# Splitting the value products of an attention stage over the two partition halves of a PSUM bank

## The chip, the cores and the metric

The kernel runs on one core of a Trainium2 chip. The metric is the device time of one execution in microseconds. The core has TensorE (PE, with weight loads shown apart as PEld), VectorE (DVE), ScalarE (ACT), GpSimd (POOL), and DMA queues that SyncE (SP), ACT and POOL issue to. PE writes only to PSUM (the tile `PS`, 128 partitions by 8 banks of 512 fp32), and DVE and ACT carry results from there to SBUF.

## The reference, cut to what matters

One inference step of a two-layer decoder trunk: a prompt of 1024 tokens with 16 meta tokens ahead of it (1040 rows), and 8 sample sequences of 8 new tokens with 512 cached ones. Layer 0 has a convolution branch and a forgetting attention of 8 heads with 64 channels; layer 1 has a short convolution and causal pooling. Each is followed by a LayerNorm and a SwiGLU feed-forward part. The change touches the prompt's attention alone:

```
s = q @ k.T / 8 + (c_q - c_k)        # c: running sum of the log forget gates
s = where(pos_k <= pos_q, s, -inf)
p = softmax(s)
out = p @ v                          # 64 columns a head
```

## The kernel before, in words

All work is placed by hand: each engine has one list of instructions, and semaphores order the engines among each other. Projections and feed-forward products (lines 688 to 690) are three fp32r matmuls for each product; they take most of the time, before and after the attention stage.

The attention stage is a loop over 80 units, ten for each head, which every engine runs through in its own list. Within a head the order is `ORDER = (0, 1, 2, 3, 4, 5, None, 6, 8, 7)`: a number i is query tile i of the prompt (128 queries, the last of them, i = 8, 16 queries) against key tiles 0 to i; `None` is one sample sequence. Unit u of head h is 10 h + its place, so units 40 to 49 belong to head 4. I write scores(u), peak(u) and so on for unit u's instructions. In step n of the loop the engines do this, in this order:

- PE: scores(n) (lines 847 to 851; for a sample sequence lines 864 to 866); transposes of the probabilities of unit n-2 (line 893); in some steps transposes of cached keys (line 873) and other small products; values(n-3) (line 914, for a sample sequence line 904).
- DVE: the reciprocal of the sum of unit n-1 (line 1686); peak(n), the row maximum (line 1682); a copy of transposed probabilities of unit n-2 to `PT` (line 1695); in some steps a piece of the convolution's norm (line 1751); in the steps 6, 7 and 9 of a head a piece of the next head's queries and keys, `head_low` (lines 1504 and 1711 with 1040 columns, line 1714).
- ACT: exp(n) to `PB` (line 1193); a copy of transposed probabilities (line 1200) or of cached keys to `KTS` (line 1205); in some steps a square for the convolution's norm (line 1267); copy(n-3), the result out of PSUM (line 1222, for a sample sequence line 1220); in the steps 5 to 8 of a head a piece of the next head (line 1239).
- POOL: normalising `PB` of unit n by the reciprocal (line 583).

Transposes and values are fp32. A value product of unit u has the key tile's 128 by 64 values as weights and 128 by m probabilities moving (m is 128, or 16 for i = 8), and adds over the i + 1 key tiles into partitions 0 to 63 of bank 7. One such product stands as two records in the trace. Bank 7 is the only one for values:

```
pe.wait_ge(att_evac, u + 1)     # ahead of values(u): the unit before has left bank 7
dve.wait_ge(exp_done, u + 3)    # ahead of the reciprocal of unit u
gp.wait_ge(rc_ready, u + 1)     # ahead of the normalising of unit u
```

`att_evac` counts the copies of line 1222. After the 80 units DVE takes reciprocals of the convolution's norm (`inverse_conv`, line 1733) and splits the first weights of the output projection into a high and a low part (`split_centred`, line 1515, after ACT's line 1112); then PE begins the output projection.

Of the kernel before, what the change touches and what calls it, by code (L numbers as in the profile page):

```python
# [10 lines left out]
ALU = mybir.AluOpType  # L11
# [3 lines left out]
P = 128  # L15
# [10 lines left out]
NH, HD = 8, 64  # L26
# [46 lines left out]
NU = NH * len(ORDER)  # L73
# [26 lines left out]
def build(nc, t):  # L100

    ctx = ExitStack()
    with ctx:
        def at(name, off, shape, dt=F32):
            n = int(np.prod(shape[1:])) * 4
            assert off % 32 == 0 and off + n <= 229344, (name, off, n)
            return nc.alloc_sbuf_tensor_at(name, shape, dt, offset=off), (off + n + 31) // 32 * 32

        def sem(name):
            return ctx.enter_context(nc.semaphore(name))  # L110

# [12 lines left out]
        AH, o = at("AH", A0, [P, KT, T], F32R)
# [15 lines left out]
        WFH, o = at("WFH", o, [P, KT, NH], F32R)  # L140
        WFL, o = at("WFL", o, [P, KT, NH], F32R)
        LFR, o = at("LFR", o, [P, NPAGE, NS, NH])

        HH, o = at("HH", B0, [P, 2, T], F32R)
        HL, o = at("HL", o, [P, 2, T], F32R)
        Y, o = at("Y", o, [P, KT, T])
        SQ, o = at("SQ", R0, [P, KT, C])
        RSD, o = at("RSD", o, [P, 2, C])
        YSM, _ = at("YSM", R0 + 21984, [P, 2, C])
        YSV, o = at("YSV", o, [P, 2, 2, C])  # L150
        assert o <= R0 + 26400

        SQA, o = at("SQA", B0 + 8 * T * 4, [P, HT, C])
        YSA, o = at("YSA", o, [P, 2, C])
        assert o <= R0

        XIN, o = at("XIN", B0, [P, XB, D])
        XTT, o = at("XTT", o, [P, TB, KT, P])
        PIN, o = at("PIN", o, [R_ALL, HALF])
        SIN, o = at("SIN", o, [P, 2, HALF])  # L160
        assert o <= B0 + 11 * T * 4

        STG, o = at("STG", A0, [P, 4, HALF])
        LFZ, o = at("LFZ", o, [NH, 3, T])
        LFC, o = at("LFC", o, [NH, TP])
        LCH, o = at("LCH", o, [NH, TP], F32R)
        LCL, o = at("LCL", o, [NH, TP], F32R)
# [3 lines left out]
        PB, o = at("PB", A0, [P, 3, TP])  # L171
        RSV, o = at("RSV", o, [P, NC, C])
        assert o <= A0 + 4 * T * 4
        QS1, o = at("QS1", A0 + 4 * T * 4, [P, 2, TP], F32R)
        assert o <= A0 + 6 * T * 4
        QS2, o = at("QS2", A0 + 6 * T * 4, [96, 2, TP], F32R)
        VP, o = at("VP", o, [P, 2, NTT, P])
        PT, o = at("PT", o, [P, 2, 8 * P])
        assert o <= A0 + 12 * T * 4
        RS, o = at("RS", B0 + 10 * T * 4, [64, HALF])  # L180
        KS1, o = at("KS1", A0 + 12 * T * 4, [P, 2, TP], F32R)
        assert o <= A0 + 14 * T * 4
        KS2, o = at("KS2", A0 + 14 * T * 4, [96, 2, TP], F32R)
        assert o <= B0

        KR, o = at("KR", 37504, [P, NPAGE, HALF])
        VR, o = at("VR", o, [P, NPAGE + 1, HALF])
        KTS, o = at("KTS", o, [P, HT, KS])
        QBD, o = at("QBD", o, [P, 328])
        SLS, o = at("SLS", o, [P, 64])  # L190
        QBA, o = at("QBA", o, [32, TP])
        assert o <= A0

        IDR, o = at("IDR", R0 + 24992, [P, P], F32R)
# [10 lines left out]
        MIX, o = at("MIX", B0, [P, HT, ES + T + EP])  # L205
        YEXT, BG, PEXT = MIX[:, :, 0:ES], MIX[:, :, ES:ES + T], MIX[:, :, ES + T:]
        assert (ES + T + EP) * 4 <= 4 * T * 4
        T1, o = at("T1", o, [P, EP + 1])
        T2, o = at("T2", o, [P, EP + 1])
        DH, o = at("DH", o, [P, T], F32R)  # L210
        WMR, _ = at("WMR", o, [P, HT, P])
        DL, o = at("DL", o, [P, T], F32R)
        OSA, o = at("OSA", o, [P, HALF])
        OSB, o = at("OSB", o, [NS * HS, HALF])
        CMP, o = at("CMP", o, [P, NS * HS + NS * NQ])
        assert o <= R0 + 26400
        WMH, o = at("WMH", R0 + 29344, [P, HT, P], F32R)
        WML, o = at("WML", o, [P, HT, P], F32R)
# [3 lines left out]
        PS = ctx.enter_context(nc.psum_tensor("PS", [P, 8, 512], F32))  # L222
# [50 lines left out]
        qk_done, nm_ready, exp_done, rc_ready, pn_ready = (sem("qk_done"), sem("nm_ready"), sem("exp_done"),  # L273
                                                           sem("rc_ready"), sem("pn_ready"))
        ta_done, tb_done, pta_ready, ptb_ready = sem("ta_done"), sem("tb_done"), sem("pta_ready"), sem("ptb_ready")
        pv_done, att_evac, sb_done, sb_evac = sem("pv_done"), sem("att_evac"), sem("sb_done"), sem("sb_evac")
        lfr_in, lfs_in, sel_in, cs_ready, cq_ready, sel_ready = (
            sem("lfr_in"), sem("lfs_in"), sem("sel_in"), sem("cs_ready"), sem("cq_ready"), sem("sel_ready"))
        kr_in, vr_in, kt_new, qbd_zero, qbd_ready, sls_ready = (sem("kr_in"), sem("vr_in"), sem("kt_new"), sem("qbd_zero"),
# [75 lines left out]
        def chunk(c):  # L355
            return slice(c * C, (c + 1) * C)
# [22 lines left out]
        def _(sp):  # L379
# [73 lines left out]
            def residual(k):  # L453

                sp.dma_start(Y[:, k, :], XT[:, k, :]).then_inc(y_in[k], 16)
# [21 lines left out]
            for k in range(KT):  # L477
                if k == 6:
                    sp.wait_ge(sb_evac, NS)
                residual(k)  # L480
            for n in range(4, 8):
                load(2 * ST_OUT0 + n, (2 * ST_OUT0 + n) % 4, out_rows(0, n))
# [199 lines left out]
        def _(pe):  # L682
# [214 lines left out]
            def values(u, h, i, m, n, na, nb):  # L897
                pe.wait_ge(att_evac, u + 1)
                if i is None:
                    pe.wait_ge(pta_ready, na + 2)  # L900
                    pe.wait_ge(vr_in, 80 * (h + 1))
                    for g in range(NPAGE + 1):
                        kw = P if g < NPAGE else NQ
                        mm = pe.matmul(PS[0:64, 7, :], PT[0:kw, u % 2, 64 * g:64 * g + 64], VR[0:kw, g, :], start=(g == 0), stop=(g == NPAGE))  # L904
                    mm.then_inc(pv_done, 1)
                    return
                if u % 20 == 0:
                    pe.wait_ge(vp_ready[h // 2 % 2], 32 * (h // 4 + 1))
                pe.wait_ge(pta_ready, na + (2 if i == 8 else 1) + 1)
                if i > 3:  # L910
                    pe.wait_ge(ptb_ready, nb + 2)
                for jt in range(i + 1):
                    kw = min(P, TP - jt * P)
                    mm = pe.matmul(PS[0:HD, 7, 0:m], VP[0:kw, h // 2 % 2, jt, HD * (h % 2):HD * (h % 2 + 1)], PT[0:kw, u % 2, m * jt:m * jt + m],  # L914
                                   start=(jt == 0), stop=(jt == i))
                mm.then_inc(pv_done, 1)

            def turn_back(s):
# [168 lines left out]
        def _(act):  # L1087
# [129 lines left out]
            def result(u, h, i, m, n, na, nb):  # L1217
                act.wait_ge(pv_done, u + 2)
                if i is None:
                    act.copy(RS[:], PS[0:64, 7, :]).then_inc(att_evac, 1)  # L1220
                else:
                    act.activation(QKV[HD * (h % 2):HD * (h % 2 + 1), h // 2, i * P:i * P + m], PS[0:HD, 7, 0:m], ACT.Copy).then_inc(att_evac, 1)

# [264 lines left out]
        def _(dve):  # L1488
# [9 lines left out]
            def two(ap):  # L1498

                return ap.unsqueeze(1).to_broadcast([P, 2, C])  # L1500
# [187 lines left out]
            def turned(u, h, i, m, n, na, nb):  # L1688
# [8 lines left out]
                if i == 8:  # L1697
                    dve.wait_ge(ta_done, na + 2)
                    dve.tensor_copy(PT[0:META, u % 2, 8 * m:9 * m], PS[0:META, 5, 0:m]).then_inc(pta_ready, 1)

            dve.wait_ge(ab_open, 1)
            def head_low(h, part):

# [31 lines left out]
            for n in range(NU + 3):  # L1735
                if 1 <= n < NU + 1:
                    inverse(*UNITS[n - 1])
                if n < NU:
                    peak(*UNITS[n])
                if 2 <= n < NU + 2:  # L1740
                    turned(*UNITS[n - 2])
                if n == 1:
                    select()
                c = norm_step(n, 13)
                if c is None:
                    c = norm_step(n, 14)
                if c is not None:
                    q = n % 10 - 3
                    qs = slice(2 * q, 2 * q + 2)
                    dve.wait_ge(la_mean, c + 1)  # L1750
                    dve.tensor_tensor(AEXT[:, qs, chunk(c)], AEXT[:, qs, chunk(c)], two(PS[:, 2, 0:C]), ALU.subtract).then_inc(la_cen, 1)
                if n < NU - 10 and n % 10 in (6, 7, 9):
                    head_low(n // 10 + 1, (6, 7, 9).index(n % 10))
                if n > NU:
                    inverse_conv(n - NU - 1)
# [360 lines left out]
```

## Time and profile before

| | us |
|---|---|
| median of 3 runs | 2765.15 (2763.03 to 2765.69) |
| the profiled execution, its own time | 2763.57 |
| its span, first to last instruction | 2761.9 |
| PE busy in the span | 2639.9 (96%) |
| stretch 336 to 633 us, steps 5 to 82 of the attention | 297.00, PE busy 286.99 |
| value products (line 914) in it, PE busy | 88.07 |
| mean granted TensorE clock, span | 0.982 |

A row of the timeline gives the start, the time from there to the end of a run of like instructions, the engine, line and operation, and in brackets the engine's idle time before and what ended it. Ends of matmuls are modelled, so the pace of a run of matmuls is read from its starts.

### The profile page before, as it was taken

How to read it: one execution, taken by the hardware profiler on the slowest of the kernel's cores; microseconds unless marked ns; L12 is line 12 of the kernel's file. 1: busy time of each engine (PE TensorE's matmuls, PEld its weight loads, DVE VectorE, ACT ScalarE, POOL GpSimd, SP SyncE). 2: the span in 40 equal slices, each digit the busy share in tenths (PEclk: the TensorE clock that was granted, in tenths of full speed). 3: DMA queues.
4: the chain of work that ended last, by engine and by line, in shares of the span. 5: the costliest groups of instructions: out<-in, count | busy, mean ns of one | idle time of the engine just before them, and what ended most of it. 6: DMA issues, size and time to landing. Idle time of an engine off the chain costs nothing.

```text
span 2761.9 us, 38352 instructions
## 1 busy us (share of the span) xinstructions
PE 2639.9 (96%) x15605; PEld 2513.8 (91%) x15605; DVE 1341.3 (49%) x1990; ACT 732.3 (27%) x1250; POOL 412.8 (15%) x415
## 2 busy tenths in 40 slices
PE   8999699998899999999999999999999999999996
PEld 7999476668899999999999999988999999999995
DVE  4788654547763333333334644577433333333355
ACT  4110355544341111111111531225211111111114
POOL 3299122223200000000002200032000000000023
PEclk9999799999999999999999999999999999999998
DMA  7210411221021111111111131121111111111101
GB/s 230 50 31 31 134 55 62 69 81 63 16 62 39 46 40 46 47 46 47 36 41 46 51 100 46 36 102 39 46 47 47 42 36 46 47 39 39 47 16 65
DMA packets 165325, 152.55 MB, mean 55 GB/s; under 512 B 8609, under 2 KB 140049, under 8 KB 165144
## 3 DMA queue, kind: packets, MB, share of 16 engines
q1 hardware_dynamic: 157632, 133.92, 16.1%
q0 software_dynamic: 6208, 15.94, 1.8%
q8 instruction: 133, 2.18, 0.3%
q10 hardware_dynamic: 1320, 0.24, 0.1%
q14 instruction: 32, 0.26, 0.0%
HBM read 131.43 MB, written 18.93 MB: 54 GB/s over the span
## 4 chain that ended last, share of the span: by engine, by line
PE 91%; DVE 5%; issue 2%; ACT 1%; DMA 1%; SPq 0%; DVEq 0%; POOL 0%; ACTq 0%
PE PS L688 26%; PE PS L689 26%; PE PS L690 26%; PE PS L914 3%; PE PS L904 1%; PE PS L893 1%; PE PS L847 1%; PE PS L864 1%; PE PS L851 1%; DVE SPR L1610 1%; DVE AL L1504 1%; DVE RSD L1787 1%; PE PS L702 0%; PE PS L703 0%; PE PS L873 0%
## 5 line engine op out<-in xcount | busy, mean ns | idle before, releaser
L688 PE MATMUL PS<-AH,WHI 128*128 128x368 f32 x3360 | 1123.3, 334 | 34.4 <-DVE Y L1850 13.4
L689 PE MATMUL PS<-AL,WHI 128*128 128x368 f32 x3360 | 1116.2, 332 | 0.0
L690 PE MATMUL PS<-AH,WLO 128*128 128x368 f32 x3360 | 1112.4, 331 | 0.0
L688 PEld LDWEIGHTS PS<-AH,WHI 128*128 128x128 f32 x3360 | 636.2, 189 | 44.2 <-DVE Y L1850 16.0
L689 PEld LDWEIGHTS PS<-AL,WHI 128*128 128x128 f32 x3360 | 635.3, 189 | 3.0 <-issue 0.8
L690 PEld LDWEIGHTS PS<-AH,WLO 128*128 128x128 f32 x3360 | 635.7, 189 | 0.0
L1880 DVE TENSOR_TENSOR HF<-S,PS 128x368 f32<-128x368 f32 x132 | 70.9, 537 | 698.5 <-ACT S L1127 698.5
L688 PE MATMUL PS<-HH,WHI 128*128 128x368 f32 x1056 | 350.2, 332 | 3.3 <-DVE Y L1891 3.2
L689 PE MATMUL PS<-HL,WHI 128*128 128x368 f32 x1056 | 349.9, 331 | 0.0
L690 PE MATMUL PS<-HH,WLO 128*128 128x368 f32 x1056 | 349.6, 331 | 0.0
L1891 DVE TENSOR_TENSOR Y<-Y,PS 128x368 f32<-128x368 f32 x480 | 251.6, 536 | 156.5 <-PE PS L690 156.5
L1127 ACT ACTIVATE S<-PS 128x368 f32<-128x368 f32 x156 | 74.7, 479 | 898.3 <-PE PS L690 898.2
L616 POOL TENSOR_TENSOR YSM<-Y 128x736 f32<-128x736 f32 x12 | 22.6, 1887 | 1546.0 <-DVE Y L1891 1429.3
L1504 DVE TENSOR_TENSOR WLO<-RAW,WHI 128x1024 fp32r<-128x1024 f32 x164 | 198.7, 1241 | 21.6 <-ACT WHI L1403 18.1
L1403 ACT CAST WHI<-RAW 128x1024 fp32r<-128x1024 f32 x108 | 107.9, 1047 | 374.6 <-PE PS L690 374.6
L688 PEld LDWEIGHTS PS<-HH,WHI 128*128 128x128 f32 x1056 | 198.8, 188 | 5.1 <-DVE Y L1891 4.8
L690 PEld LDWEIGHTS PS<-HH,WLO 128*128 128x128 f32 x1056 | 198.9, 188 | 0.0
L689 PEld LDWEIGHTS PS<-HL,WHI 128*128 128x128 f32 x1056 | 198.5, 188 | 0.2
L1682 DVE TENSOR_REDUCE ST<-PS 128x1 f32<-128x128 f32 (+4 forms) x80 | 63.7, 796 | 127.0 <-PE PS L851 81.4
L1598 DVE SCALAR_TENSOR_TENSOR PS<-AEXT,PRT,PS 128x1040 f32<-128x1040 f32 x87 | 113.4, 1303 | 2.3
L1504 DVE TENSOR_TENSOR HL<-HF,HH 128x368 fp32r<-128x368 f32 x132 | 77.1, 584 | 74.8 <-ACT HH L1382 74.8
L1850 DVE TENSOR_TENSOR Y<-Y,PS 128x368 f32<-128x368 f32 x144 | 75.2, 533 | 53.6 <-PE PS L690 53.4
(255 smaller groups left out, 2295.0 us busy)
## 6 DMA issues: line engine op xcount, KB each, us to landing
RAW<-in_w_ffn_gate SPq DMA_DIRECT2D x44, 512.0 KB, 4.0
RAW<-in_w_ffn_up SPq DMA_DIRECT2D x44, 512.0 KB, 4.9
RAW<-in_w_ffn_down SPq DMA_DIRECT2D x44, 512.0 KB, 3.5
RAW<-in_w_in_even SPq DMA_DIRECT2D x20, 512.0 KB, 4.9
Y<-x_spill SPq DMA_DIRECT2D x16, 552.0 KB, 5.3
KR<-in_cache_k SPq DMA_DIRECT2D x32, 256.0 KB, 3.2
VR<-in_cache_v SPq DMA_DIRECT2D x32, 256.0 KB
RAW<-in_w_in_odd SPq DMA_DIRECT2D x16, 512.0 KB, 4.9
```

The lines of the kernel that those rows point to most:

```text
L688: pe.matmul(out, wh, xh, start=first, stop=False)
L689: pe.matmul(out, wh, xl, start=False, stop=False)
L690: return pe.matmul(out, wl, xh, start=False, stop=last)
L914: mm = pe.matmul(PS[0:HD, 7, 0:m], VP[0:kw, h // 2 % 2, jt, HD * (h % 2):HD * (h % 2 + 1)], PT[0:kw, u % 2, m * jt:m * jt + m], start=(jt ...
L1127: act.activation(s_tile[:, par, :] if bank0_to is None else bank0_to, PS[:, 2 * par, 0:C], func).then_inc(s_ready, 1)
L1403: act.copy(WHI[:, 2 * s1 % 4 + e, :], RAW[:, 2 * s1 % 4 + e, :]).then_inc(w_hi, 1)
L1504: return dve.tensor_tensor(out, x, f32(hi), ALU.subtract)
L1598: dve.scalar_tensor_tensor(acc, src, row(k, R_DW + j), acc, ALU.mult, ALU.add).then_inc(acc_step, 1)
L1682: dve.tensor_reduce(ST4[0:m, 0, u:u + 1], src, AX_X, ALU.max, negate=True).then_inc(nm_ready, 1)
L1850: dve.tensor_tensor(y, y, PS[:, 4 + n % 3, 0:C], ALU.add).then_inc(d_free, 1)
L1880: dve.tensor_tensor(HF[:, par, :], S[:, par, :], PS[:, 2 * par + 1, 0:C], ALU.mult).then_inc(gu_free, 1)
L1891: dve.tensor_tensor(y, y, PS[:, 4 + n % 3, 0:C], ALU.add).then_inc(d_free, 1)
```

## The change: key tiles alternate between partition halves

Value products of even key tiles still write partitions 0 to 63 of bank 7; those of odd key tiles write partitions 64 to 127. Each half is a sum of its own. Query tile 0 has one key tile and is carried out as before. For the other query tiles ACT copies the upper half to a new SBUF tile `PVT` (signalled by `pv_half`), and DVE adds it to the lower half in PSUM and writes the sum to `QKV`; this addition is what counts up `att_evac`. DVE's addition for unit n-3 stands in step n after the copy to `PT` and the norm's piece, and ahead of `head_low`. SP waits for all results before the last two tiles of the residual.

```
         PVT, o = at("PVT", o, [HD, P])
...
             for k in range(KT):
                 if k == 6:
                     sp.wait_ge(sb_evac, NS)
+                    sp.wait_ge(att_evac, 1 + NU)
                 residual(k)
...
                 for jt in range(i + 1):
                     kw = min(P, TP - jt * P)
-                    mm = pe.matmul(PS[0:HD, 7, 0:m], VP[...], PT[...],
-                                   start=(jt == 0), stop=(jt == i))
+                    half = slice(HD * (jt % 2), HD * (jt % 2 + 1))
+                    mm = pe.matmul(PS[half, 7, 0:m], VP[...], PT[...],
+                                   start=(jt < 2), stop=(jt > i - 2))
                 mm.then_inc(pv_done, 1)
...
                 act.wait_ge(pv_done, u + 2)
                 if i is None:
                     act.copy(RS[:], PS[0:64, 7, :]).then_inc(att_evac, 1)
+                elif i:
+                    act.copy(PVT[:, 0:m], PS[HD:P, 7, 0:m]).then_inc(pv_half, 1)
                 else:
                     act.activation(QKV[...], PS[0:HD, 7, 0:m], ACT.Copy).then_inc(att_evac, 1)
...
+            def gathered(u, h, i, m, n, na, nb):
+                if i is None or i == 0:
+                    return
+                dve.wait_ge(pv_half, 8 * h + u % 10 - (u % 10 > 6))
+                dve.tensor_tensor(QKV[...], PS[0:HD, 7, 0:m], PVT[:, 0:m],
+                                  ALU.add).then_inc(att_evac, 1)
...
+                if n >= 3:
+                    gathered(*UNITS[n - 3])
                 if n < NU - 10 and n % 10 in (6, 7, 9):
                     head_low(n // 10 + 1, (6, 7, 9).index(n % 10))
                 if n > NU:
                     inverse_conv(n - NU - 1)
```

DVE's list in the steps 46 to 48 of a head such as head 4, before (`KS` and `QS` are the next head's keys and queries, `ST` holds maxima and sums):

```order
L1682 TENSOR_REDUCE ST_112<-PS 64x1
L1695 COPY PT<-PS 128x512
L1504 TENSOR_TENSOR KS_100<-QKV,KS_99 64x1040
L1686 RECIPROCAL ST_112<-ST_112 64x1
L1682 TENSOR_REDUCE ST_112<-PS 128x1
L1695 COPY PT<-PS 128x512
L1711 SCALAR_TENSOR_TENSOR QS_94<-QKV,QS_94 64x1040
L1686 RECIPROCAL ST_112<-ST_112 128x1
L1682 TENSOR_REDUCE ST_112<-PS 16x1
```

and the same place now, where line numbers have moved by a few (1687 is the peak, 1691 the reciprocal, 1700 the copy to `PT`):

```order
L1687 TENSOR_REDUCE ST_113<-PS 64x1
L1700 COPY PT<-PS 128x512
L1711 TENSOR_TENSOR QKV<-PS,PVT 64x128
L1509 TENSOR_TENSOR KS_101<-QKV,KS_100 64x1040
L1691 RECIPROCAL ST_113<-ST_113 64x1
L1687 TENSOR_REDUCE ST_113<-PS 128x1
L1700 COPY PT<-PS 128x512
L1711 TENSOR_TENSOR QKV<-PS,PVT 64x128
L1724 SCALAR_TENSOR_TENSOR QS_94<-QKV,QS_94 64x1040
L1691 RECIPROCAL ST_113<-ST_113 128x1
L1687 TENSOR_REDUCE ST_113<-PS 16x1
```

The addition (now line 1711) has come ahead of `head_low`, the reciprocal and the next peak.

DVE's list at the end of the stage, before:

```order
L1695 COPY PT<-PS 128x64
L1699 COPY PT<-PS 16x16
L1695 COPY PT<-PS 128x512
L1733 RECIPROCAL RSV<-RSV 128x368 x2
L1515 SCALAR_TENSOR_TENSOR WLO<-RAW,WMN,WHI 128x1024 x2
```

and now:

```order
L1700 COPY PT<-PS 128x64
L1704 COPY PT<-PS 16x16
L1711 TENSOR_TENSOR QKV<-PS,PVT 64x128
L1700 COPY PT<-PS 128x512
L1711 TENSOR_TENSOR QKV<-PS,PVT 64x16
L1746 RECIPROCAL RSV<-RSV 128x368
L1711 TENSOR_TENSOR QKV<-PS,PVT 64x128
L1746 RECIPROCAL RSV<-RSV 128x368
L1520 SCALAR_TENSOR_TENSOR WLO<-RAW,WMN,WHI 128x1024 x2
```

The last additions stand ahead of each of the two reciprocals of the norm, and so ahead of the weights' split.

## Rows read from the trace of the kernel before

**Rows 1.** The page's chain that ended last, by line: share of the span.
```profile
PE PS L688 26%; PE PS L689 26%; PE PS L690 26%; PE PS L914 3%; PE PS L904 1%; PE PS L893 1%; PE PS L847 1%; PE PS L864 1%; PE PS L851 1%; DVE SPR L1610 1%; DVE AL L1504 1%; DVE RSD L1787 1%; PE PS L702 0%; PE PS L703 0%; PE PS L873 0%
```

**Rows 2.** Stretch, its length, busy PE, PEld, DVE, ACT, POOL; last row line 914.
```profile
472.57:510.25 37.68, 36.73 (x237) 25.33 (x236) 17.49 (x35) 19.66 (x48) 8.14 (x12) 1.00 0.22 72
336.00:633.00 297.00, 286.99 (x1825) 197.70 (x1823) 143.91 (x274) 159.68 (x375) 76.06 (x98) 0.99 0.22 70
...
336.00:633.00 297.00, 88.07 (x714) 71.77 (x714) 0.99 0.22 70
```

**Rows 3.** Timeline, two value passes: weight loads for 128 and for 16 moving columns.
```profile
481.06 1.72 PEld L914 LDWEIGHTS PS<-PT,VP 128*64 128x64 f32 x16 [0.52 <-issue]
...
515.06 1.22 PEld L914 LDWEIGHTS PS<-PT,VP 128*64 128x64 f32 x18 [0.17 <-issue]
```

**Rows 4.** Groups of instructions by line: two DVE forms that read PSUM.
```profile
L1880 DVE TENSOR_TENSOR HF<-S,PS 128x368 f32<-128x368 f32 x132 | 70.9, 537 | 698.5 <-ACT S L1127 698.5
...
L1695 DVE COPY PT<-PS 128x128 f32<-128x128 f32 x7 | 2.0, 281 | 0.0
```

**Rows 5.** Timeline of head 4, steps 43 to 46: peaks, ACT copies, sample scores.
```profile
483.85 0.69 DVE L1682 TENSOR_REDUCE ST<-PS 128x1 f32<-128x512 f32 x1 [3.00 <-PE PS L851]
...
487.93 0.27 ACT L1222 ACTIVATE QKV<-PS 64x128 f32<-64x128 f32 x1
...
488.24 0.96 DVE L1682 TENSOR_REDUCE ST<-PS 128x1 f32<-128x768 f32 x1 [0.47 <-PE PS L851]
...
490.12 0.58 ACT L1205 COPY KTS<-PS 128x512 f32<-128x512 f32 x1
...
490.75 3.65 PE L864 MATMUL PS<-KTS,QBD 128*64 128x512 f32 x8 [0.88 <-ACT KTS L1205]
```

**Rows 6.** Timeline of head 5, step 54, the same place.
```profile
525.93 0.96 DVE L1682 TENSOR_REDUCE ST<-PS 128x1 f32<-128x768 f32 x1 [0.23 <-PE PS L851]
...
526.47 0.27 ACT L1222 ACTIVATE QKV<-PS 64x128 f32<-64x128 f32 x1
```

**Rows 7.** Timeline of head 4, steps 46 to 49: DVE, ACT, and PE's sample values.
```profile
497.36 1.24 DVE L1504 TENSOR_TENSOR KS<-QKV,KS 64x1040 fp32r<-64x1040 f32 x1
...
498.88 1.09 DVE L1682 TENSOR_REDUCE ST<-PS 128x1 f32<-128x896 f32 x1
...
500.60 1.24 DVE L1711 SCALAR_TENSOR_TENSOR QS<-QKV,QS 64x1040 fp32r<-64x1040 f32 x1
...
501.95 1.21 DVE L1682 TENSOR_REDUCE ST<-PS 16x1 f32<-16x1040 f32 x1
...
497.45 0.24 ACT L1200 COPY PT<-PS 128x128 f32<-128x128 f32 x1
...
501.26 0.27 ACT L1222 ACTIVATE QKV<-PS 64x128 f32<-64x128 f32 x1
...
504.31 0.25 ACT L1222 ACTIVATE QKV<-PS 64x128 f32<-64x128 f32 x1
...
505.67 4.64 PE L904 MATMUL PS<-VR,PT 128*64 128x512 f32 x10
```

**Rows 8.** Timeline of the stage's end: ACT, DVE, first product of the output projection.
```profile
628.97 0.18 ACT L1222 ACTIVATE QKV<-PS 64x16 f32<-64x16 f32 x1
...
630.59 1.15 ACT L1112 ACTIVATE WHI<-RAW,WMN 128x1024 fp32r<-128x1024 f32 x1
...
626.29 4.75 DVE L1733 RECIPROCAL RSV<-RSV 128x368 f32<-128x368 f32 x2
630.96 3.74 DVE L1515 SCALAR_TENSOR_TENSOR WLO<-RAW,WMN,WHI 128x1024 fp32r<-128x1024 f32 x2
...
635.63 0.64 PE L688 MATMUL PS<-AH,WHI 128*128 128x368 f32 x1 [3.42 <-DVE WLO L1515]
```

**Rows 9.** Busy time by stretch, heads 1 and 2; granted clock third from the end.
```profile
360.30:363.60 3.30, 3.30 (x17) 2.97 (x15) 0.28 (x1) 0.27 (x1) 1.54 (x1) 0.50 0.65 227
...
398.00:401.30 3.30, 3.23 (x31) 2.87 (x31) 0.60 (x5) 1.22 (x6) 0.38 (x1) 1.00 0.87 248
```

More of the change, by code:

```diff
@@ L275, in build @@
         ta_done, tb_done, pta_ready, ptb_ready = sem("ta_done"), sem("tb_done"), sem("pta_ready"), sem("ptb_ready")
-        pv_done, att_evac, sb_done, sb_evac = sem("pv_done"), sem("att_evac"), sem("sb_done"), sem("sb_evac")
+        pv_done, att_evac, sb_done, sb_evac, pv_half = sem("pv_done"), sem("att_evac"), sem("sb_done"), sem("sb_evac"), sem("pv_half")
         lfr_in, lfs_in, sel_in, cs_ready, cq_ready, sel_ready = (
@@ L479, in _ @@
                     sp.wait_ge(sb_evac, NS)
+                    sp.wait_ge(att_evac, 1 + NU)
                 residual(k)
@@ L913, in values @@
                     kw = min(P, TP - jt * P)
-                    mm = pe.matmul(PS[0:HD, 7, 0:m], VP[0:kw, h // 2 % 2, jt, HD * (h % 2):HD * (h % 2 + 1)], PT[0:kw, u % 2, m * jt:m * jt + m],
-                                   start=(jt == 0), stop=(jt == i))
+                    half = slice(HD * (jt % 2), HD * (jt % 2 + 1))
+                    mm = pe.matmul(PS[half, 7, 0:m], VP[0:kw, h // 2 % 2, jt, HD * (h % 2):HD * (h % 2 + 1)], PT[0:kw, u % 2, m * jt:m * jt + m],
+                                   start=(jt < 2), stop=(jt > i - 2))
                 mm.then_inc(pv_done, 1)
@@ L1220, in result @@
                     act.copy(RS[:], PS[0:64, 7, :]).then_inc(att_evac, 1)
+                elif i:
+                    act.copy(PVT[:, 0:m], PS[HD:P, 7, 0:m]).then_inc(pv_half, 1)
                 else:
@@ L1699, in turned, with gathered @@
                     dve.tensor_copy(PT[0:META, u % 2, 8 * m:9 * m], PS[0:META, 5, 0:m]).then_inc(pta_ready, 1)
+            def gathered(u, h, i, m, n, na, nb):
+                if i is None or i == 0:
+                    return
+                dve.wait_ge(pv_half, 8 * h + u % 10 - (u % 10 > 6))
+                dve.tensor_tensor(QKV[HD * (h % 2):HD * (h % 2 + 1), h // 2, i * P:i * P + m], PS[0:HD, 7, 0:m], PVT[:, 0:m],
+                                  ALU.add).then_inc(att_evac, 1)
             dve.wait_ge(ab_open, 1)
@@ L1751, in _ @@
                     dve.tensor_tensor(AEXT[:, qs, chunk(c)], AEXT[:, qs, chunk(c)], two(PS[:, 2, 0:C]), ALU.subtract).then_inc(la_cen, 1)
+                if n >= 3:
+                    gathered(*UNITS[n - 3])
                 if n < NU - 10 and n % 10 in (6, 7, 9):
```

## The prediction

> **What bounds the kernel now.** I read the chain that ended last first: PE work leads nearly everywhere, and the value products of line 914 hold 3% of the span in it [rows 1]. Then the attention stage by stretch: PE is busy 286.99 of 297.00 us, DVE 143.91 and ACT 159.68, and the value products take 88.07 of PE's time [rows 2]. So PE bounds this stage, and what the change cuts from PE comes off the time as long as nobody else becomes late. DVE and ACT have half of the stage free on average, but an average does not tell where; that needs the timeline of one head, step by step, and of the stage's end.
>
> **What PE may save.** A pass of 16 records with 128 moving columns starts a weight load every 0.105 us ((1.72 - 0.14)/15, the last load being 0.14 long); one of 18 records with 16 columns starts one every 0.064 us ((1.22 - 0.14)/17) [rows 3]. The loads are alike (128x64), so 0.064 is what loads alone allow, and the 128 columns set the 0.105. If products in the two halves stream side by side, the columns are shared out to two halves (0.053 a record) and the loads become the limit: 0.041 less for each record. I take that. Without overlap the saving is nothing; with loads side by side as well it is half of either pace. A head has 70 records in tiles i = 1 to 7: 2.9 us, 23 us in eight heads. The pass of i = 8 keeps its pace.
>
> The Trainium skill, in "TensorE: Matmul & The Clock Gate" (Part 3: Packing small matmuls), says that products in different column groups run concurrently, and gives 2.38x for three such tiles. By that alone two halves would at best halve the 88 us. The same skill, in "TensorEngine Tiling (Array Packing)" (PSUM Bottleneck), warns that packing speeds up TensorE and not the way out of PSUM. No row of this trace shows products in two column groups; what follows weighs the way out by rows.
>
> **What the way out costs.** Before, copy(n-3) took 0.27 us on ACT and freed bank 7. Now ACT's copy, of the same size, is followed by DVE's addition. Its price lies between 0.18 (ACT's copy of 16 columns [rows 8]) and 0.54 (DVE's addition of 368 columns from PSUM and SBUF); it is nearest to DVE's copy of 128 columns, 0.28, which I take, and the line through the two gives 0.16 for 16 columns [rows 4]; a hand-over between engines takes 0.03. The price matters less than the place: the addition waits for ACT, and behind it in DVE's list stand `head_low`, the reciprocal (for which POOL waits) and the next peak (for which ACT's exp waits). A step then has a ring across both engines: peak(n), exp(n), ACT's copies up to copy(n-3), the addition, `head_low`, peak(n+1). Before, peak(n+1) needed PE's scores and DVE's own earlier work, not ACT's copies.
>
> I walk through head 4. Steps 40 to 42: the passes of i = 6 (14 records) and i = 7 (16) save 0.57 and 0.66, so step 43 begins 1.23 early. The additions hold nothing here: DVE idles 3.00 us before peak(43) [rows 5].
>
> Steps 44 and 45: copy(41) starts at 487.93 behind ACT's other copies, not behind PE, and ends at 488.20. The addition ends at 488.51, the reciprocal follows, and peak(45), 0.11 behind the addition, starts at 488.62, where it stood at 488.24: +0.38. Through exp(45) and the copy to `KTS` of 490.12 this reaches the sample scores, which wait for that copy at 490.75 [rows 5]. So the sample scores start 1.23 - 0.38 = 0.85 early; what PE saves in between it waits away. In heads 1, 3 and 5 ACT also has a square ahead of copy(n-3): in head 5 it starts at 526.47, ends at 526.74, and peak(55) comes at 527.16 and not 525.93 [rows 6]: +1.23, all that was won.
>
> Steps 46 to 49, as if the sample scores had not moved: values(43) now ends 0.33 earlier, and copy(43) runs behind ACT's copy of 497.45, at about 497.61 to 497.88. The addition ends at 498.19, `head_low` (1.24) at 499.46, and peak(47) starts 0.11 later (as 501.84 to 501.95), at 499.57 and not 498.88: +0.69. That shift passes through exp(47) to copy(44): 501.95 to 502.22; addition to 502.53; the second `head_low` (500.60 before) to 503.80; peak(48) at 503.91 and not 501.95: +1.96. Through exp(48) copy(45) moves to 506.27 and ends at 506.52; its addition ends at 506.83, and only then may the sample's values start: 506.86 and not 505.67 [rows 7], +1.2. Their 4.64 us let DVE and ACT catch up, so the next head starts with this shift alone.
>
> The sum over heads. Head 0 has no passes before step 3, so no early start: +0.4 + 1.2 = +1.6. Heads 1, 3, 5: 0 + 1.2 each, +3.6. Heads 2, 4, 6: -0.85 + 1.2 each, +1.05. Head 7 has no `head_low`, and PE keeps its own savings of 0.33 + 0.41 in the passes of i = 3 and 4: -0.85 - 0.75 = -1.6. Together +4.65.
>
> The stage's end: the 16-column copy(78) ends at 629.15; its addition (0.16 by that line) at 629.34. Only then may the first reciprocal of `inverse_conv` start, which stood at 626.29. Copy(79) stands behind ACT's work to 631.74 and ends at 632.04, its addition at 632.35, and behind that the second reciprocal (2.4) ends at 634.8. So the weights' split starts at 634.8 and not 630.96, and the first product that waits for it at 639.4 and not 635.63 [rows 8]: +3.8.
>
> The wait added to SP's list costs nothing: the residual's tiles 6 and 7 then leave at about 632.4, and the output rows they are added to come many products behind the first.
>
> Total +4.65 + 3.8 = +8.4. The profiled execution took 2763.57 us, 1.6 below the median of the runs; +8.4 gives 2772.0 and 2773.6. I forecast 2773 us, 0.3% slower. A change within 0.2% (5.5 us) could hardly be told from none.
>
> **The rivals.**
>
> (a) No overlap: records keep 0.105. Then no step starts early, and copy(43) stays at 497.75 (+0.14 on the ring). Heads 2, 4, 6: 0.38 + 1.34 = 1.72 each; heads 1, 3, 5: 1.23 + 1.34 = 2.57 each; head 0: 1.7; head 7: 0.5; end: 3.8 + 0.7, since values(79) ends later. Total +19.6: 2785. For it: no row shows overlap. Chance 0.2.
>
> (b) Loads side by side too: 0.0525 and 0.032 a record. Steps 40 to 42 save 0.73, 0.58 and 0.84, 0.9 more than above in each of heads 1 to 7, -6.4 in all: 2767, no change that can be told. The Trainium skill's "TensorEngine Tiling (Array Packing)" (Key Properties) says that tiles load and multiply in parallel; by that rule it would be this case. Chance 0.17.
>
> (c) The other side: the ring is not late. If DVE's and ACT's step stays shorter than PE's, PE keeps all 23 us and pays the end: 2765.15 - 23 + 3.8 = 2746. It turns at the ring's length: peak(47) to peak(48) is 4.34 us in my walk, against 3.07 between these peaks before [rows 7], so my reading of the lists would have to be wrong by more than 1.27 us a step. Chance 0.1.
>
> (d) The clock. In head 1, where PE's records are nearly gapless, the granted clock was 0.50 in one stretch of 3.3 us and stayed at 1.00 in the like stretch of head 2 [rows 9]. That is 1.2 instead of 2.4 GHz and costs at most 1.65 us. PE now waits more: about 1.6 us ahead of the sample scores and 1 to 2 us in steps 48 and 49. Four such stretches more add 6.6: 2780. Chance 0.15.
>
> **How the numbers follow.** My walk holds with 0.38, at 2773 with about 4 us to each side (the addition's price alone, four times on the ring in six heads, gives -3 to +6). Slower by over 0.2%: 0.29 of the walk's 0.38, 0.2 of (a), 0.13 of (d), 0.03 of (b), together 0.65. Same: 0.08 + 0.02 + 0.13 = 0.23. Faster: 0.01 + 0.01 + 0.1 = 0.12. The range from 2761 to 2788 holds all of (a), (b) and (d) and leaves (c) out; the walk's own is 2769 to 2777.
>
> **What would show it.** Line 914's records pace at 0.064 or below if the halves overlap, at 0.105 if not. From one head's first scores to the next's head 4 should take some 0.35 us longer than its 37.68 [rows 2], head 5 some 1.2 us longer than its own; PE should wait for the new addition ahead of the values of i = 5 and of the sample, and the first reciprocal of `inverse_conv` should start right behind the 16-column addition. PE busy in the stage should fall by 20 us while its idle time grows by more. The prediction is wrong if DVE shows no wait for ACT's `PVT` copy ahead of its peaks, or if the step 47 to 48 stays at 3 us.

## The result, and the profile after

The changed kernel takes 2776.39 us (median of 6 runs, 2774.96 to 2781.24), the kernel before took 2765.42 us beside it (2763.03 to 2769.37): a ratio of their means of 1.0042, 95% interval 1.0029 to 1.0055. It is 0.4% slower, 11 us. The profiled execution has a span of 2773.3 us against 2761.9.

First the page's chain of the kernel after, by engine and then by line, which answers to [rows 1] (the value products are line 917 now, the copy to `PVT` 1225, the addition 1711, peak 1687, exp 1196).

```profile
PE 86%; DVE 7%; ACT 3%; issue 2%; DMA 1%; SPq 0%; DVEq 0%; POOL 0%; ACTq 0%
PE PS L690 26%; PE PS L691 26%; PE PS L692 26%; PE PS L866 1%; ACT PB L1196 1%; PE PS L906 1%; DVE ST L1687 1%; PE PS L917 1%; DVE AL L1509 1%; PE PS L698 1%; DVE SPR L1615 1%; DVE RSD L1802 1%; PE PS L849 1%; PE PS L895 1%; PE PS L705 0%
```

The value products have gone from 3% of the chain to 1%, and exp and peak have come into it. Busy time by stretch (the stage, then head 2 from its first peak to that of the next head, then line 917 alone), which answers to [rows 2]:

```profile
338.00:644.00 306.00, 266.04 (x1821) 169.15 (x1818) 154.29 (x338) 162.26 (x378) 74.43 (x98) 0.96 0.20 65
401.93:439.56 37.63, 33.19 (x237) 21.41 (x237) 19.02 (x44) 20.02 (x49) 8.13 (x12) 1.00 0.23 71
...
338.00:644.00 306.00, 57.60 (x714) 41.01 (x714) 0.96 0.20 65
```

Line 917 takes 57.60 us, not 88.07, so the halves do overlap; yet a head lasts 37.63 us, as before, and PE is busy for 33.19 of it instead of 36.7. The loads and products of two passes on the timeline, to be held against [rows 3]:

```profile
405.49 0.76 PEld L917 LDWEIGHTS PS<-PT,VP 128*64 128x64 f32 x18 [0.17 <-issue]
408.73 0.85 PEld L917 LDWEIGHTS PS<-PT,VP 128*64 128x64 f32 x16 [0.52 <-issue]
...
408.73 1.09 PE L917 MATMUL PS<-PT,VP 128*64 128x128 f32 x16
```

Sixteen records start one every 0.047 us ((0.85 - 0.14)/15), eighteen of 16 columns one every 0.036 ((0.76 - 0.14)/17). Where the time went is seen in steps 27 and 28 of head 2, the same place as [rows 7], on the timeline:

```profile
426.84 1.06 DVE L1687 TENSOR_REDUCE ST<-PS 128x1 f32<-128x896 f32 x1
...
427.94 1.01 ACT L1196 ACTIVATE PB<-PS,ST 128x896 f32<-128x896 f32 x1 [1.70 <-DVE ST L1687]
...
428.94 0.36 ACT L1203 COPY PT<-PS 128x256 f32<-128x256 f32 x1
429.32 0.26 ACT L1225 COPY PVT<-PS 64x128 f32<-64x128 f32 x1
...
429.62 0.28 DVE L1711 TENSOR_TENSOR QKV<-PS,PVT 64x128 f32<-64x128 f32 x1 [1.12 <-ACT PVT L1225]
429.93 1.24 DVE L1724 SCALAR_TENSOR_TENSOR QS<-QKV,QS 64x1040 fp32r<-64x1040 f32 x1
429.96 0.88 PE L917 MATMUL PS<-PT,VP 128*64 128x128 f32 x12 [0.83 <-DVE QKV L1711]
...
431.28 1.21 DVE L1687 TENSOR_REDUCE ST<-PS 16x1 f32<-16x1040 f32 x1
```

Read it as a ring: peak, exp, ACT's two copies, the addition after 1.12 us of waiting, `head_low`, the next peak: 4.44 us from peak to peak, where the same two peaks stood 3.07 apart before. PE waits 0.83 us for the addition on the way. The sums over the stage, from the waits (us in total, times, longest):

```profile
ACT PB L1196 <- DVE ST L1687: 112.3, 75, 5.8
DVE QKV L1711 <- ACT PVT L1225: 83.4, 63, 2.7
...
PE PS L866 <- ACT KTS L1208: 13.9, 8, 1.9
...
PE PS L917 <- DVE QKV L1711: 10.2, 13, 2.3
```

VectorE waits for ScalarE and ScalarE for VectorE; what TensorE saved is among its waits, for the key copies `KTS` and the addition above all.

The second thing to see is the clock. Here are a stretch of head 1 and the one behind it (granted clock third from the end), and the sample scores that fall into the first:

```profile
378.70:382.12 3.42, 3.15 (x4) 0.98 (x5) 0.45 (x2) 2.17 (x4) 0.91 (x1) 0.50 0.48 171
382.12:399.19 17.07, 14.60 (x95) 8.68 (x94) 10.35 (x18) 8.45 (x17) 4.55 (x4) 1.00 0.00 1
```
```profile
378.97 5.19 PE L866 MATMUL PS<-KTS,QBD 128*64 128x512 f32 x8 [1.90 <-ACT KTS L1208]
```

The eight records took 5.19 us, at 1.2 GHz for most of it, where they took 3.65 before [rows 5]; PE had just waited 1.90 us. Both kernels begin the stage with one stretch of 20.5 us at half clock. Besides it, the heads held one such stretch of 3.41 us before; now they hold six. Last, the stage's end, against [rows 8], with the last peak of before (line 1682) and of after (line 1687) ahead of it:

```profile
616.85 1.23 DVE L1682 TENSOR_REDUCE ST<-PS 128x1 f32<-128x1024 f32 x1 [0.48 <-PE PS L851]
```
```profile
626.84 1.19 DVE L1687 TENSOR_REDUCE ST<-PS 128x1 f32<-128x1024 f32 x1
...
638.46 0.17 DVE L1711 TENSOR_TENSOR QKV<-PS,PVT 64x16 f32<-64x16 f32 x1 [2.26 <-ACT PVT L1225]
638.66 2.45 DVE L1746 RECIPROCAL RSV<-RSV 128x368 f32<-128x368 f32 x1
...
641.15 0.28 DVE L1711 TENSOR_TENSOR QKV<-PS,PVT 64x128 f32<-64x128 f32 x1
...
641.46 2.45 DVE L1746 RECIPROCAL RSV<-RSV 128x368 f32<-128x368 f32 x1
...
643.83 3.74 DVE L1520 SCALAR_TENSOR_TENSOR WLO<-RAW,WMN,WHI 128x1024 fp32r<-128x1024 f32 x2
...
648.51 0.65 PE L690 MATMUL PS<-AH,WHI 128*128 128x368 f32 x1 [7.85 <-DVE WLO L1520]
```

From the last peak to the first product of the next stage it is 21.67 us, against 18.78.

### The profile page after: what moved, and what is told of

Same layout as the page of the kernel before. It is cut to its first block, busy times and chain, and to the rows that moved or that the text cites. A ratio compares the mean times of both kernels' runs of the same rounds, so it can differ in the third digit from the quotient of the medians.

```text
span 2773.3 us, 38417 instructions
## 1 busy us (share of the span) xinstructions
PE 2616.4 (94%) x15605; PEld 2481.2 (89%) x15605; DVE 1356.8 (49%) x2054; ACT 732.7 (26%) x1250; POOL 413.1 (15%) x415
## 4 chain that ended last, share of the span: by engine, by line
PE 86%; DVE 7%; ACT 3%; issue 2%; DMA 1%; SPq 0%; DVEq 0%; POOL 0%; ACTq 0%
PE PS L690 26%; PE PS L691 26%; PE PS L692 26%; PE PS L866 1%; ACT PB L1196 1%; PE PS L906 1%; DVE ST L1687 1%; PE PS L917 1%; DVE AL L1509 1%; PE PS L698 1%; DVE SPR L1615 1%; DVE RSD L1802 1%; PE PS L849 1%; PE PS L895 1%; PE PS L705 0%
## 5 line engine op out<-in xcount | busy, mean ns | idle before, releaser
L1509 DVE TENSOR_TENSOR WLO<-RAW,WHI 128x1024 fp32r<-128x1024 f32 x164 | 199.1, 1244 | 21.7 <-ACT WHI L1408 18.1
L585 POOL TENSOR_SCALAR PB<-PB,ST 128x128 f32<-128x128 f32 (+4 forms) x80 | 62.4, 780 | 232.4 <-DVE ST L1691 232.4
```

Source lines behind the costliest of these rows:

```text
L585: gp.tensor_scalar(PB[0:m, u % 3, 0:n], PB[0:m, u % 3, 0:n], ST4[0:m, 2, u:u + 1], 1.0, ALU.mult, ALU.mult).then_inc(pn_ready, 1)
L1509: return dve.tensor_tensor(out, x, f32(hi), ALU.subtract)
```

## The experiments

Three theories were tried against each other. A: the halves make TensorE faster, and the addition's place in VectorE's list takes it back. B: it is the work of the way out, not the place (or, where only the products changed, they are worth nothing). C: it is the clock. The table gives each kernel's time, its ratio to the kernel before on the same chip (95% interval), the profiled execution's time from peak(0) to peak(79) with TensorE's mean granted clock there, and an even and an odd head at full clock. A head marked ~ held a half-clock stretch; the 1.4 to 1.7 us by which the step with the stretch is longer than the same step without is taken off. Each kernel has one profiled execution. From the first product of the next stage on, code that no edit touches took 2118 to 2130 us in eleven of the twelve, and 2139 with the wait filled; so the heads say more of an edit than the total does.

| kernel | time, us | ratio | peak 0 to 79 | clock | even head | odd head |
|---|---|---|---|---|---|---|
| before | 2765.4 | | 292.6 | 0.98 | 37.7 | 37.7 |
| the change | 2776.4 | 1.0042 (1.0029 to 1.0055) | 300.5 | 0.95 | 37.6 | ~38.2 |
| products only | 2747.9 | 0.9940 (0.9927 to 0.9953) | 272.2 | 0.97 | 34.3 | 35.0 |
| way out only | 2789.7 | 1.0086 (1.0073 to 1.0099) | 310.0 | 0.96 | 39.2 | 39.8 |
| addition behind `head_low` | 2775.5 | 1.0034 (1.0020 to 1.0048) | 302.6 | 0.91 | ~35.6 | ~37.3 |
| reciprocals first at the end | 2772.8 | 1.0024 (1.0015 to 1.0033) | 305.3 | 0.94 | 37.6 | ~38.2 |
| addition behind peak | 2775.0 | 1.0029 (1.0016 to 1.0042) | 309.4 | 0.92 | ~37.6 | under 39.3 |
| way out only, behind peak | 2797.2 | 1.0114 (1.0096 to 1.0132) | 322.8 | 0.98 | 41.3 | 41.6 |
| two copies, late addition | 2762.0 | 0.9992 (0.9979 to 1.0004) | 287.2 | 0.95 | 35.2 | 37.3 |
| addition twice | 2793.4 | 1.0109 (1.0091 to 1.0128) | 318.4 | 0.92 | 38.4 | ~39.6 |
| wait filled | 2796.6 | 1.0106 (1.0092 to 1.0119) | 308.7 | 0.91 | 37.8 | 38.2 |
| two copies, spread additions | 2757.0 | 0.9968 (0.9956 to 0.9980) | 281.7 | 0.95 | ~34.6 | 35.7 |

### The products alone

```
# kernel before, with the products of the change; way out as before
+ half = slice(HD * (jt % 2), HD * (jt % 2 + 1))
+ mm = pe.matmul(PS[half, 7, 0:m], ...)
  act.activation(QKV[...], PS[0:HD, 7, 0:m], ACT.Copy).then_inc(att_evac, 1)
```

> Products through both halves as in the change, but the way out of before: ScalarE copies the lower half alone to its place, so the sums of the odd key tiles are left out of the output; no second copy, no addition. Theory A (the halves do make TensorE faster, and the addition's place in VectorE's list takes it back): the products of the stage fall from 88 us of TensorE to some 58, heads come at about 35 us instead of 37.7, the time is 2738 to 2750. Theory B (the faster products are worth nothing, because the stage waits for peaks and exponentials anyway): 2762 to 2767. Theory C (the clock: a TensorE that is less busy gets more half-clock stretches, whatever the way out): the six stretches of 3.41 us at granted clock 0.5 are there here too, time 2752 to 2760.

It took 2747.9 us, 17.5 less than before. Here are heads 2 and 3, by stretch:

```profile
392.05:426.32 34.27, 33.03 (x237) 21.40 (x237) 17.26 (x35) 19.54 (x49) 8.10 (x12) 1.00 0.26 78
426.32:461.35 35.03, 33.16 (x237) 21.40 (x237) 19.42 (x38) 21.14 (x50) 11.54 (x14) 1.00 0.20 62
```

PE is busy as long as in the change (33.19 us in a head there), but the head is over in 34.27 us. So the faster products are worth 3.4 and 2.7 us a head, and the way out of the change costs 3.4 and 3.2. The time is within A's range. B falls for this kernel, and C too: the heads hold two half-clock stretches, 10.2 us in all, not six.

### The way out alone

```
# the change, with products as before, all to PS[0:HD, 7, 0:m]
+ act.copy(PVT[:, 0:m], PS[0:HD, 7, 0:m]).then_inc(pv_half, 1)
+ dve.tensor_tensor(QKV[...], PS[0:HD, 7, 0:m], PVT[:, 0:m], ALU.max).then_inc(att_evac, 1)
```

> Products as before, all to the lower half; the way out of the change: ScalarE copies the lower half to the buffer, VectorE takes the larger of bank and buffer (the same number twice), so the output is whole. Theory A: TensorE has no gain to pay with, each step keeps its pace and the ring over peak, exponential, copy and addition is added where it is late: 2779 to 2792. Theory B: the added instructions cost little in themselves, since ScalarE and VectorE are about half idle: 2765 to 2772. Theory C (clock): few half-clock stretches, as TensorE stays as busy as before, 2766 to 2775.

At 2789.7 us it is 24 over before, within A's range. The profiled execution, 2779.1, was its fastest; the others are 2788.6 to 2790.1. In the profiled one the heads take 17.4 us more than before and the stage's end 4.8, but the code behind takes 8.3 less; where the others spent their 10 us no trace shows. At full clock heads grow by 1.5 and 2.1 us, less than the 3.4 and 3.2 that the way out costs behind fast products: a TensorE that takes longer hides part of the ring. Four heads also begin with a half-clock stretch. This is the case of the prediction's rival (a), which put it at 2785.

### The addition behind the next head's low parts

```
+ if n < NU - 10 and n % 10 in (6, 7, 9):
+     head_low(n // 10 + 1, (6, 7, 9).index(n % 10))
  if n >= 3:
      gathered(*UNITS[n - 3])
- if n < NU - 10 and n % 10 in (6, 7, 9):
-     head_low(n // 10 + 1, (6, 7, 9).index(n % 10))
```

> The change with one swap in VectorE's list: at places 6, 7 and 9 of a head the low parts for the next head (about 1.24 us twice) stand ahead of the addition, not behind it, so they fill VectorE's wait for the copy. Theory A: the ring is shorter by up to 1.24 us at two steps of seven heads, at most 17 us; since VectorE's wait there is about as long as the piece, 2762 to 2772. Theory B (the price is the work, not the place): 2774 to 2779. Theory C: as B, unless the half-clock stretches go.

2775.5 us, no different from the change. Yet the ring did shorten, as A has it. VectorE in head 2:

```profile
426.29 1.06 DVE L1687 TENSOR_REDUCE ST<-PS 128x1 f32<-128x896 f32 x1
427.28 0.67 DVE L1700 COPY PT<-PS 128x512 f32<-128x512 f32 x1
427.98 1.24 DVE L1724 SCALAR_TENSOR_TENSOR QS<-QKV,QS 64x1040 fp32r<-64x1040 f32 x1
429.25 0.28 DVE L1711 TENSOR_TENSOR QKV<-PS,PVT 64x128 f32<-64x128 f32 x1
429.46 0.14 DVE L1691 RECIPROCAL ST<-ST 128x1 f32<-128x1 f32 x1
429.53 1.21 DVE L1687 TENSOR_REDUCE ST<-PS 16x1 f32<-16x1040 f32 x1
```

The low part fills what was the wait for the copy, and peak to peak is 3.24 us, not 4.44. Seven heads gain some 2 us (even) or 1 (odd). But over the same 80 steps the mean granted clock is 0.91 and not 0.95: the stage holds 44 us at half clock inside the heads instead of 20.5. The time is in B's range, but not for B's reason: the place counts, and the clock took back what it gave.

### The reciprocals ahead of the last additions

```
+ if n > NU:
+     inverse_conv(n - NU - 1)
  if n >= 3:
      gathered(*UNITS[n - 3])
- if n > NU:
-     inverse_conv(n - NU - 1)
```

> The change with the reciprocals of the norm (2.45 us each) ahead of the last two additions in VectorE's list. Theory A: in the change two of them stand behind waits of 2.26 and 2.29 us and ahead of the split that the next stage's first product waits for; ahead of the additions they fill these waits: 4 to 5 us less, 2771 to 2773. The rival: the reciprocals hold back the additions, the last products start later by as much and ScalarE's copies of the next stage wait for the sums instead: 2776 to 2779.

2772.8 us, within A's range, but the trace bears out only part of it. VectorE at the stage's end, and the first product behind it:

```profile
639.91 2.44 DVE L1746 RECIPROCAL RSV<-RSV 128x368 f32<-128x368 f32 x1
642.39 0.17 DVE L1711 TENSOR_TENSOR QKV<-PS,PVT 64x16 f32<-64x16 f32 x1
...
649.95 0.65 PE L690 MATMUL PS<-AH,WHI 128*128 128x368 f32 x1 [5.36 <-DVE WLO L1520]
```

The wait of 2.26 us ahead of the 16-column addition is gone. It was the only one that the reciprocals could fill: the last addition had none in the change, where it ran right behind the first reciprocal (641.15); the 2.29 of the expectation was a wait of TensorE. From the last peak (630.64) to the first product it is 19.31 us, 2.4 less than in the change. The time is 3.6 us lower, and the two intervals overlap. No row ties what is more than 2.4 to this edit: in the profiled execution the heads are 4.8 us longer than in the change (27.3 us at half clock, not 20.5), and the code behind is 3.7 shorter. So that the time fell within A's range is partly luck.

### The addition behind the next peak, with either kind of product

```
  if n < NU:
      peak(*UNITS[n])
+ if 4 <= n < NU + 3:
+     gathered(*UNITS[n - 4])
  ...
- if n >= 3:
-     gathered(*UNITS[n - 3])
```

> The change with the addition of unit n-3 put one place later in VectorE's list: behind peak(n+1), ahead of the PT copy, so that it no longer stands between exp(n) and peak(n+1); the way out is the same work. Products alone through the halves left heads of 34.3 and 35.0 us, the change has 37.6 and more. Theory A (the place): TensorE finds its bank free about 0.3 us after each peak, while its own transposes run, so heads come at 35 to 36 us, 2749 to 2760. Theory B (the work itself, a copy and an addition in a row before the bank is free): heads stay at 37.5, 2772 to 2778. Theory C (clock): the heads get shorter and the half-clock stretches take it back, as with the addition behind the next head's low parts, where heads that held none were some 2 us shorter and the time stayed at 2775.

> The same late place for the addition with the products as before, all to the lower half (VectorE takes the larger of bank and buffer, the same number twice). The early place cost 24 us here. Theory A: with TensorE at its old pace the way out is hidden, 2763 to 2769. Theory B: the way out still costs most of its 24 us, 2780 to 2790.

2775.0 and 2797.2 us: A fails in both, and the second is above B's range too. The waits of the first say why (stretch 330:630; in the change the second row is 7.6, 11, 0.8):

```profile
PEld PS L917 <- DVE QKV L1711: 34.1, 42, 1.7
PE PS L917 <- DVE QKV L1711: 24.7, 39, 1.6
```

There are two rings, not one. VectorE's list is the first. The second is bank 7: values(n-3) can't start before unit n-4 has left it. With the addition behind the peak, TensorE makes scores, waits for VectorE to reduce them and then to add, and only then may write the next values: a row from head 2,

```profile
430.73 0.87 PE L917 MATMUL PS<-PT,VP 128*64 128x128 f32 x10 [0.78 <-DVE QKV L1711]
```

ends a wait that the early place does not have there. B describes this rightly: a copy and an addition, in a row, before the bank is free. With the slow products the heads take 41.3 and 41.6 us, some 2 us more than with the addition in its early place. None of the three places tried for this addition suits both rings.

### Two copies on ScalarE, and the addition a step later

```
- act.copy(PVT[:, 0:m], PS[HD:P, 7, 0:m]).then_inc(pv_half, 1)
+ act.wait_ge(pv_sum, k - 2)      # where k > 2
+ act.copy(PVT[own, k % 2, 0:m], PS[HD:P, 7, 0:m])
+ act.activation(QKV[...], PS[0:HD, 7, 0:m], ACT.Copy).then_inc(att_evac, 1)
  ...
  # VectorE, behind peak(n+1):
+ dve.tensor_tensor(out, out, PVT[own, k % 2, 0:m], ALU.add).then_inc(pv_sum, 1)
```

> Products through both halves; ScalarE copies both halves out (the upper to a buffer of two slots, the lower to its place) and frees the bank with the second copy; VectorE adds the buffer to the place a step later, behind peak, and nothing in the stage waits for it but the buffer's slot. Theory A: the addition leaves the ring altogether, ScalarE's second copy adds some 0.3 us a step to an engine that is half idle, heads of 34.5 to 36 us, 2746 to 2756. Theory B: ScalarE's copies stand ahead of the next exponential and take the ring's place: 2765 to 2776. Theory C (clock): more half-clock stretches than the five of the products alone, 2755 to 2765.

2762.0 us: out of both rings, heads come at 35.2 and 37.3 us. The even ones are A's; the odd ones are not, the clock is at 0.95, and the time is in C's range. Its heads hold three half-clock stretches, 20.5 us in all; those of the products alone held two, not the five that C names. Two rows of head 3, VectorE's and GpSimd's:

```profile
461.62 1.72 DVE L1720 TENSOR_TENSOR QKV<-QKV,PVT 64x128 f32<-64x128 f32 x1
...
461.43 1.75 POOL L597 TENSOR_TENSOR YSA<-SQA 128x736 f32<-128x736 f32 x1
```

The same addition takes 0.27 to 0.38 us nearly everywhere else (one at the stage's end takes 1.43, beside another two-input instruction of GpSimd). Its two inputs now come from SBUF, and it ends 0.16 us behind GpSimd's sum for the norm; heads 1 and 5 have the same pair of rows. Behind it stand a PT copy and `head_low`.

### The addition twice

```
+ dve.tensor_tensor(PVX[:, 0:m], PS[0:HD, 7, 0:m], PVT[:, 0:m], ALU.add).then_inc(pv_sum, 1)
  dve.tensor_tensor(QKV[...], PS[0:HD, 7, 0:m], PVT[:, 0:m], ALU.add).then_inc(att_evac, 1)
```

> The change with each addition done twice in the early place, the first time into a spare buffer: 0.28 us more in the ring at seven of ten steps (0.17 at the narrow one). Theory A (the ring sets the pace at the steps where VectorE waits for the copy and TensorE for VectorE, about three to five of ten): 8 x (3 to 5) x 0.28 = 7 to 11 us more than the change, 2783 to 2788. Theory B (VectorE's work is hidden, only the clock costs): 2773 to 2779.

2793.4 us, 17 more than the change and more than A had. In the trace the second addition starts 0.20 us behind the first:

```profile
434.81 0.28 DVE L1715 TENSOR_TENSOR PVX<-PS,PVT 64x128 f32<-64x128 f32 x1 [1.12 <-ACT PVT L1226]
435.01 0.27 DVE L1716 TENSOR_TENSOR QKV<-PS,PVT 64x128 f32<-64x128 f32 x1
```

Four steps of an even head are 0.20 us longer (4.64 instead of 4.44, for one) and four of an odd head 0.3, which makes a head 0.8 and 1.4 us longer at full clock: the ring sets the pace at four of ten steps. With heads 0 and 7 that is some 9 us, as A has it; nearly all of the rest is half clock, 44 us in the heads instead of 20.5. B falls.

### TensorE's wait filled

```
# two waits that stood behind now stand ahead of these products
+ for _ in range(2 if s % 2 else 0):
+     pe.matmul(PS[0:64, base, 0:PAST], SLS[:], KBS[:, 0:PAST], start=True, stop=True)
  pe.wait_ge(ptb_ready, NB_KEYS[s, HT - 1] + 2)
```

> The change with two products of 512 columns (a finished pair of operands, into the bank that the sample scores overwrite) that TensorE does in odd heads ahead of its wait of 1.9 us for the last key copy. Theory C (TensorE's waits bring the half-clock stretches, and those of odd heads' sample scores cost 1.6 us each): three of the six stretches of the stage go, the sample step of odd heads falls from 9.4 to 7.8 us, 2770 to 2773. The rival (a stretch doesn't hang on that wait): the stretches stay or move, and the step keeps its 9.4 us or grows by up to 0.4, 2775 to 2780.

At its place the edit did what C says. Head 1, the two products and the sample scores behind them:

```profile
377.05 1.88 PE L861 MATMUL PS<-KBS,SLS 128*64 128x512 f32 x4
379.11 3.65 PE L868 MATMUL PS<-KTS,QBD 128*64 128x512 f32 x8 [0.18 <-ACT KTS L1210]
```

3.65 us again, not 5.19, and the sample step takes 7.8 us in all four odd heads, where three of them had 9.3 to 9.5 in the change. But stretches now fall elsewhere (even heads' sample steps of 9.6 us, stretches of 10.24 us in heads 3 and 7): the heads hold 47.8 us at half clock instead of 20.5. The total is 2796.6, outside both ranges.

The profiled execution is 21.7 us longer than that of the change: 8.1 of it in the heads and 14.5 behind the first product of the next stage (2139.4 us to the end, 2124.8 in the change), in code that is the same but for its position. TensorE stops there with nothing to wait for, as the waits from 990 to 1330 us show:

```profile
PE PS L692 <- issue: 7.1, 3, 2.6
PE PS L690 <- issue: 5.0, 3, 1.8
```

The stops of the second row stand in the change too (4.6 us), those of the first do not. At each of the three new stops a half-clock stretch begins, 13.7 us in all, in which products start every 0.31 us instead of 0.17. Together that is some 14 of the 14.5 us; what brings the stops is not shown. So filling the wait removed the stretches at these three places, but it did not leave fewer in the heads, and the run does not settle what the time would be without any.

### Two copies, and the additions where VectorE is idle

```
  # PVT with four slots, ScalarE as with the late addition; VectorE:
  inverse(*UNITS[n - 1])
+ for k in {0: (7, 6, 5), 6: (4,)}.get(n % 10, ()):
+     gathered(*UNITS[n - k])
  peak(*UNITS[n])
  ...
+ if n % 10 in (1, 2, 3, 5):          # end of the step
+     gathered(*UNITS[n - 4])
```

> As the late addition with two copies by ScalarE, with four slots in the buffer and the additions where VectorE has been seen idle: three at the head's first step and one at the sample step, ahead of a peak that TensorE is still making, the rest at the end of steps 1, 2, 3 and 5. None stands in steps 6 to 9, where the late addition cost 0.2 us each in even heads and 1.72 us in odd ones, beside GpSimd's sum of the norm. Theory A (VectorE's list is what is left of the price): heads of 34.3 to 34.6 us even and 35.0 to 35.5 odd without half-clock stretches, 2747 to 2755. Theory B (ScalarE's second copy is the price): heads stay at 35.2 and 37.3, 2758 to 2766. Theory C: heads shorten where the clock is full, but stretches take it back, 2755 to 2762.

2757.0 us, 0.3% less than before and 0.7% less than the change: of the versions that leave nothing out, the one that beats both. Heads 2 and 3:

```profile
396.08:432.31 36.23, 34.54 (x237) 22.85 (x237) 19.30 (x43) 22.20 (x57) 8.34 (x12) 0.95 0.22 74
432.31:468.04 35.73, 33.20 (x237) 21.41 (x237) 21.94 (x46) 23.05 (x58) 11.73 (x14) 1.00 0.19 61
```

The heads are A's to within 0.3 us, the time is C's: heads 2, 4 and 6 hold a half-clock stretch at their start, head 7 one of 10.24 us. A second bank for the products, so that the addition holds nobody up, was not tried.

## Why the prediction came out as it did

The forecast was 2773 us, slower; 2776.4 was measured. The mechanism is the one that was walked through: the addition of 0.28 us (0.17 at 16 columns), the ring from peak(47) to peak(48) of 4.44 us where 4.34 was worked out, VectorE's wait for the copy, PE's waits ahead of the values of i = 5 and of the sample. Without the addition (and without the odd key tiles' sums) the same products and copies give 2747.9, and with the additions moved to idle places of VectorE's list, at the price of a second copy on ScalarE, the whole result takes 2757.0: the cost is the addition and where it stands. Rival (c) is out, and (a) too, since line 917 fell to 57.60 us.

Two sizes were off, in opposite directions. **The saving** was put at 0.041 us a record with 128 columns and none at 16; the measured paces of 0.047 and 0.036 make it 0.058 and 0.028, a little more at 128 columns than rival (b) had. The Trainium skill's "TensorEngine Tiling (Array Packing)" (Key Properties), by whose rule (b) was to come, is borne out by these loads. **The clock**, rival (d), came on top; the walk had it at nothing. By heads, from the first peaks, the change against before:

| head | walk | measured | less half-clock |
|---|---|---|---|
| 0 | +1.6 | +1.6 | +1.6 |
| 1, 3, 5 | +1.2 each | +0.5, +2.3, +2.3 | +0.5, +0.6, +0.6 |
| 2, 4, 6 | +0.35 each | -0.1, +1.5, +1.5 | -0.1, 0.0, -0.1 |
| 7 | -1.6 | -1.7 | -1.7 |
| sum | +4.65 | +8.0 | +1.5 |

In the last column the 1.5 to 1.7 us by which a step with a stretch is longer than its like are taken off, in head 1 on both sides. With the faster pace the heads are 3.1 us better than the walk, half of what (b) counted on; five stretches in the heads (the sixth, in head 5, lengthens no step) against one before cost 6.5, where (d) put four more at 6.6. That they hang together with PE's waits was a rival's guess. The filled wait bears it out at the odd heads' sample scores alone: there the stretches went, but more came elsewhere. What decides where and how many there are stays open.

**The end** was put at +3.8 and is +2.9: the first reciprocal does start right behind the 16-column addition, and the run with the reciprocals ahead takes 2.4 of it back. The 16-column addition ended 11.8 us behind the last peak, not 12.5, and the last addition did not have to wait for its copy. The sum: 8.0 + 2.9, and 0.5 from code that is the same (peak(0) stands 2.0 later, the rest takes 1.5 less): 11.4, as the spans have it. So the mechanism was right, but that the total came within 3.4 us of the forecast is partly luck: 4.0 us too much in the walk's heads and end stand against 6.5 of the clock.

## What to carry to other kernels

A cheaper product is worth only what the way out of its bank leaves of it: before the edit, follow both the in-order list of each engine that frees the bank and the bank itself, since a place that suits the one may stall the other. Let one engine free the bank, and do the rest of the work later, in stretches where the trace shows its engine waiting for the bound engine. And where TensorE is given waits, look at the granted clock before judging an edit: here one that shortened the steps by up to 2 us a head gained nothing.

## What had not been expected of the hardware

VectorE's addition took 0.28 us with one input in PSUM, 0.29 with both in SBUF, and 1.72 with both in SBUF beside GpSimd's two-input sum of 1.75; the Trainium skill's "GPSIMD Engine Reference" (1. Specifications) says that the two share their way to SBUF and contend when a VectorE instruction has two SBUF inputs, which the 1.72 us agree with. That the place of the input decides is seen in the run with the addition behind the peak: with one input in PSUM it stood in the midst of the same sum and took 0.28 us.

```profile
386.42 1.75 POOL L596 TENSOR_TENSOR YSA<-SQA 128x736 f32<-128x736 f32 x1
386.67 0.28 DVE L1711 TENSOR_TENSOR QKV<-PS,PVT 64x128 f32<-64x128 f32 x1
```

Two inputs in SBUF do not always cost beside GpSimd: of the spread additions, three in a row took 1.54 us in odd heads and 0.67 in even ones, each time beside the same normalising instruction of GpSimd (heads 1 and 2):

```profile
393.28 1.54 DVE L1720 TENSOR_TENSOR QKV<-QKV,PVT 64x128 f32<-64x128 f32 x3
393.41 1.27 POOL L586 TENSOR_SCALAR PB<-PB,ST 128x1024 f32<-128x1024 f32 x1 [1.64 <-DVE ST L1698]
...
429.53 0.67 DVE L1720 TENSOR_TENSOR QKV<-QKV,PVT 64x128 f32<-64x128 f32 x3
```

The half-clock time of the heads varied widely between kernels that differ little: one stretch of 3.41 us before, and nine, 44 us in all, in a run that differs from the change only in the order of VectorE's list. In the run with sixteen more TensorE records, stops of up to 2.6 us in "issue" came at three places half a millisecond later, where the change has none; that they come from the code's new position is not shown. Products in the two halves of PSUM loaded their weights side by side as well: 1.72 us became 0.85 for sixteen loads, 1.22 became 0.76 for eighteen.
